# Router from unscaled rows, its broadcasts in two parts, and the first expert loaded in six pieces

## The reference

```
x = x + merged @ w_out
h = rmsnorm(x, g_ffn)                  # x * rsqrt(mean(x*x) + eps) * g
g_prob = softmax(h @ w_rg + b_rg)      # 4 groups; the best one
e_sel  = (h @ w_re + b_re)[group]      # 8 experts of that group
p_e, e_idx = top_k(softmax(e_sel), 2)  # two experts a row, shares scaled to sum 1
for e in range(32):
    hid = silu(h @ w_gate[e]) * (h @ w_up[e])          # 1024 -> 512
    y  += (hid * dense_w[:, e:e+1]) @ w_down[e]        # 512 -> 1024
x = x + y
```

## Time and profile before

| | before |
|---|---|
| median of 3 runs | 1783.94 us (1783.86 to 1784.62) |
| the profiled execution: its time | 1780.57 us |
| its span, first to last instruction | 1778.8 us |
| TensorE busy | 1538.4 us (86%) |
| VectorE busy | 945.3 us (53%) |
| ScalarE (ACT) busy | 633.7 us (36%) |
| bytes moved, mean rate | 407.85 MB, 229 GB/s |
| experts' gate/up loads: number, size, median from issue to landing | 32, 4096 KB, 37.9 us |
| mean granted TensorE clock | 0.937 |

### The profile page before, as it was taken

The page is one execution under the profiler, slowest core; times in us unless marked ns, Lnnn a source line. Parts: engine busy times, 40 slices in busy tenths (PEclk is TensorE's granted clock), DMA queues, the critical chain, the costliest instruction groups (busy, mean ns, idle before and its releaser), DMA issues.

```text
span 1778.8 us, 30446 instructions
## 1 busy us (share of the span) xinstructions
PE 1538.4 (86%) x12249; PEld 1257.9 (71%) x12250; DVE 945.3 (53%) x1717; ACT 633.7 (36%) x1026; POOL 58.5 (3%) x71
## 2 busy tenths in 40 slices
PE   7999997999999999997999997996859666666666
PEld 7999886799989999885899986885744333333233
DVE  5666686466566666775665667764643222222222
ACT  5444564444444444563544457434310000000000
POOL 1000020000000000010200000000000000000000
PEclk9999998999999999998999998998979988888888
DMA  9555362265565554550555543442099999999996
GB/s 310 188 188 186 127 223 83 72 213 172 188 200 159 193 184 165 169 184 26 184 189 183 189 165 101 134 151 77 15 418 393 430 430 431 431 430 432 434 428 297
DMA packets 147225, 407.85 MB, mean 229 GB/s; under 512 B 5216, under 2 KB 98768, under 8 KB 138976
## 3 DMA queue, kind: packets, MB, share of 16 engines
q1 hardware_dynamic: 145888, 404.31, 61.3%
q0 software_dynamic: 1280, 2.75, 0.7%
HBM read 406.00 MB, written 1.05 MB: 229 GB/s over the span
## 4 chain that ended last, share of the span: by engine, by line
PE 60%; DMA 19%; DVE 9%; issue 5%; ACT 5%; POOL 1%; SPq 0%; POOLq 0%; DVEq 0%; ACTq 0%
DMA expert_gu<-in_exp_gu 19%; PE bank L1869 17%; PE bank L1870 17%; PE bank L1871 17%; PE bank L2448 4%; DVE wlo L1128 2%; ACT whi L702 2%; POOL small L627 1%; ACT prob L811 1%; PE bank L2464 1%; PE bank L2203 1%; DVE x L1185 1%; PE bank L2411 1%; ACT xn L716 1%; ACT hhi L710 0%
## 5 line engine op out<-in xcount | busy, mean ns | idle before, releaser
L1128 DVE TENSOR_TENSOR wlo<-raw,whi 128x1024 fp32r<-128x1024 f32 (+1 forms) x396 | 449.5, 1183 | 150.6 <-ACT whi L702 149.8
L1869 PE MATMUL bank<-hhi,whi 128*128 128x256 f32 x1504 | 427.7, 284 | 8.7 <-DVE hlo L1166 4.3
L1870 PE MATMUL bank<-hlo,whi 128*128 128x256 f32 x1504 | 426.6, 284 | 0.0
L1871 PE MATMUL bank<-hhi,wlo 128*128 128x256 f32 x1504 | 426.6, 284 | 0.0
L702 ACT ACTIVATE whi<-raw 128x1024 fp32r<-128x1024 f32 (+1 forms) x396 | 382.3, 1019 | 92.6 <-PE bank L1871 92.5
L1869 PEld LDWEIGHTS bank<-hhi,whi 128*128 128x128 f32 x1504 | 289.4, 192 | 13.0 <-issue 5.2
L1870 PEld LDWEIGHTS bank<-hlo,whi 128*128 128x128 f32 x1504 | 289.6, 193 | 3.1
L1871 PEld LDWEIGHTS bank<-hhi,wlo 128*128 128x128 f32 x1504 | 289.5, 192 | 0.0
L2448 PE MATMUL bank<-expert_gu,h_e 128*32 128x256 f32 x2112 | 169.9, 492 | 130.6 <-DMA expert_gu<-in_exp_gu 126.4
L2448 PEld LDWEIGHTS bank<-expert_gu,h_e 128*32 128x32 f32 x2112 | 84.6, 140 | 215.8 <-issue 194.4
L1817 DVE SCALAR_TENSOR_TENSOR e_sg<-e_th,bank 128x128 f32<-128x128 f32 x33 | 9.5, 287 | 305.2 <-ACT e_th L1084 305.2
(11 more groups left out here) (358 smaller groups left out, 1652.2 us busy)
## 6 DMA issues: line engine op xcount, KB each, us to landing
expert_gu<-in_exp_gu SPq DMA_DIRECT2D x32, 4096.0 KB, 37.9
expert_dn<-in_exp_dn SPq DMA_DIRECT2D x32, 2048.0 KB, 38.7
raw<-in_ffn_w_gate SPq DMA_DIRECT2D x44, 1024.0 KB, 5.5
raw<-in_ffn_w_up SPq DMA_DIRECT2D x44, 1024.0 KB, 7.4
raw<-in_ffn_w_down SPq DMA_DIRECT2D x44, 1024.0 KB, 4.9
raw<-in_w_in SPq DMA_DIRECT2D x36, 1024.0 KB, 5.1
raw<-in_w_o SPq DMA_DIRECT2D x8, 1024.0 KB, 5.3
raw<-in_w_out SPq DMA_DIRECT2D x4, 1024.0 KB, 5.2
```

The costliest lines, as they stand in the source:

```text
L1128: nc.vector.tensor_tensor(slot_view(wlo, slot, src), src, slot_view(whi, slot, src).bitcast(F32), ALU.subtract).then_inc(lo_ready, inc)
L1869: nc.tensor.matmul(o, sh, mh, start=first, stop=False, skip_group_check=shared)
L1870: nc.tensor.matmul(o, sh, ml, start=False, stop=False, skip_group_check=shared)
L1871: return nc.tensor.matmul(o, sl, mh, start=False, stop=last, skip_group_check=shared)
```

## The change

- SP no longer waits for all six raw tiles to be free before it loads expert 0. It loads it in six pieces of 1 MB (four of gate/up, two of down), each as soon as the job that lay in that place has been split. Expert 2's down tile goes behind the first piece, its gate/up tile ahead of the last.
- The rows that TensorE turns for the router are those of x, neither scaled nor multiplied by the gain. The gain is multiplied into `w_router` instead, and the row's scale is applied to the logits. `hcol` is copied by ACT for t = 0 and by VectorE for t = 1. The squares go to a tile of their own (`sink`). `xn`, which the gather needs, is x times gain from VectorE and then scaled by ACT.
- The shares' four `diag` operations are on ACT, directly after the picks, and have a matmul of their own; the slots' four stay on VectorE, behind `take`, and their matmul stands behind the first gather. Both matmuls use one bank.
- `w_router`'s product with the gain and two memsets (`give`, `y_sb`) stand ahead of the last update of x.

The core of the diff:

```diff
@@ -592,15 +596,39 @@
-                if plan:
-                    for k in range(2):
-                        for w in last_use(last, batches(last) - 2 + k):
-                            sp.wait_ge(lo_ready, w)
-                expert(0, 0, None)
+                st, b, m = plan[last]
+                def piece(job):
+                    n = 3 * ((b + job // 3) % 2) + job % 3
+                    sp.wait_ge(lo_ready, mid_pos(last, job, 1) + 1)
+                    t, name, o, done = (expert_gu[0], "exp_gu", n, gu_landed[0]) if n < 4 else (expert_dn[0], "exp_dn", n - 4, down_landed[0])
+                    dst = t[:].rearrange("p k q n -> p (k q n)") if n < 4 else t[:].rearrange("p k n -> p (k n)")
+                    c = slice(o * 2 * HALF, (o + 1) * 2 * HALF)
+                    sp.dma_start(dst[:, c], a[name][0, :, c]).then_inc(done if o == 0 else consts_loaded, 16)
+                def down_part(e, j):
+                    src = a["exp_dn"][e:e + 1, :, :].rearrange("e p n -> p (e n)")
+                    sp.dma_start(expert_dn[j][:].rearrange("p k n -> p (k n)"), src).then_inc(down_landed[j], 16)
+                def gate_up_part(e, j):
+                    src = a["exp_gu"][e:e + 1, :, :].rearrange("e p n -> p (e n)")
+                    sp.dma_start(expert_gu[j][:].rearrange("p k q n -> p (k q n)"), src).then_inc(gu_landed[j], 16)
+                jobs = 3 * batches(last)
+                piece(jobs - 6)
+                sp.wait_ge(yt_ready, 4)
+                down_part(2, 2)
+                for job in range(jobs - 5, jobs - 1):
+                    piece(job)
...
-                expert(2, 2, None)
+                gate_up_part(2, 2)
+                piece(jobs - 1)
...
-                expert(1, 1, None)
+                gate_up_part(1, 1)
+                down_part(1, 1)
...
@@ -1064,18 +1092,31 @@
-                for g in range(4):
-                    t, h = g // 2, g % 2
-                    act.wait_ge(tr_ready, n + g + 1)
-                    nc.scalar.activation(hcol[:, 4 * h:4 * h + 4, t * P:(t + 1) * P],
-                                         TR[g][:].rearrange("p (k c) -> p k c", c=P), ACT.Copy).then_inc(hhi_ready, 1)
-                act.wait_ge(glogits_ready, 1)
-                nc.scalar.activation(g4[:, :, 1, :], g4[:, :, 0, :], ACT.Exp).then_inc(gexp_ready, 1)
-                act.wait_ge(elogits_ready, 1)
-                nc.scalar.activation(x8[:, :, 1, :], x8[:, :, 0, :], ACT.Exp).then_inc(eexp_ready, 1)
-                act.wait_ge(rows_done, 1)
-                for h in range(2):
-                    nc.scalar.activation(rows4[:, 2 * h:2 * h + 2, :].rearrange("p v c -> p (v c)"), bank[6 + h][:],
+                for t in range(T):
+                    act.wait_ge(x_ready, 4 * i + 2 * t - 2)
+                    if t:
+                        act.wait_ge(squares_ready, 2 * i + 1)
+                    nc.scalar.activation(sink[:], x[:, t, :], ACT.Square, accum_out=small[:, 0, t:t + 1]).then_inc(squares_ready, 1)
+                    for h in range(2 if t == 0 else 0):
+                        act.wait_ge(tr_ready, n + h + 1)
+                        nc.scalar.activation(hcol[:, 4 * h:4 * h + 4, 0:P], TR[h][:].rearrange("p (k c) -> p k c", c=P),
+                                             ACT.Copy).then_inc(hhi_ready, 1)
+                act.wait_ge(root_ready, roots_by(i) + 1)
+                act.wait_ge(xn_ready, T)
+                for t in range(T):
+                    nc.scalar.activation(xn[:, t, :], xn[:, t, :], ACT.Identity, scale=nr[:, 0, t:t + 1]).then_inc(xn_ready, 1)
+                act.wait_ge(expin_ready, 1)
+                nc.scalar.activation(g4[:, :, 1, :], g4[:, :, 0, :], ACT.Exp).then_inc(expout_ready, 1)
+                act.wait_ge(expin_ready, 2)
+                nc.scalar.activation(x8[:, :, 1, :], x8[:, :, 0, :], ACT.Exp).then_inc(expout_ready, 1)
+                act.wait_ge(picks_ready, 1)
+                for v_ in range(2):
+                    for t in range(T):
+                        ins = nc.scalar.activation(diag[:, 2 * (2 + v_) + t, :], ident[:], ACT.Identity, scale=one[:, t, 10 + v_:11 + v_])
+                ins.then_inc(expout_ready, 1)
+                for o in range(2):
+                    act.wait_ge(rows_done, o + 1)
+                    nc.scalar.activation(rows4[:, 2 - 2 * o:4 - 2 * o, :].rearrange("p v c -> p (v c)"), bank[7][:],
...
@@ -1688,16 +1731,19 @@
-                update_x(i, 0.5)
-            def norm_rows(i):
-                dve.wait_ge(squares_ready, 2 * i + 2)
-                r = small[:, 3, 0:T]
-                rsqrt([mean_eps(0, T, D)], T, r)
+                if not moe:
+                    update_x(i, 0.5)
+                    return
+                dve.wait_ge(route_loaded, 80)
+                nc.vector.tensor_tensor(w_router[:], w_router[:], gcols[:, i + 1, :].rearrange("p (k o) -> p k o", o=1).broadcast_to([P, KC, LOGITS]),
+                                        ALU.mult)
+                nc.vector.memset(give[:], 0.0).then_inc(give_ready, 1)
+                nc.vector.memset(y_sb[:], 0.0).then_inc(y_copied, 1)
...
-                    nc.vector.scalar_tensor_tensor(xn[:, t, :], x[:, t, :], r[:, t:t + 1], gain[:],
-                                                   ALU.mult, ALU.mult).then_inc(xn_ready, 1)
+                    update_row(i, 0.5, t)
+                    dve.wait_ge(x_ready, 4 * i + 2 * t + 2)
+                    nc.vector.tensor_tensor(xn[:, t, :], x[:, t, :], gain[:], ALU.mult).then_inc(xn_ready, 1)
...
@@ -1721,15 +1767,21 @@
-                dve.wait_ge(route_loaded, 80)
+                n = turned(i)
+                for h in range(2):
+                    dve.wait_ge(tr_ready, n + 2 + h + 1)
+                    V.tensor_copy(hcol[:, 4 * h:4 * h + 4, P:S], TR[2 + h][:].rearrange("p (k c) -> p k c", c=P)).then_inc(hlo_ready, 1)
+                dve.wait_ge(squares_ready, 2 * i + 2)
+                root([mean_eps(0, T, D)])
+                dve.wait_ge(root_ready, roots[0])
...
-                link(V.tensor_tensor(logits[:], bank[4][:, 0:T * LOGITS].rearrange("p (t n) -> p t n", t=T),
-                                     b_router[:].rearrange("p (o n) -> p o n", o=1).broadcast_to([P, T, LOGITS]), ALU.add))
+                link(*[V.scalar_tensor_tensor(logits[:, t, :], bank[6][:, t * LOGITS:(t + 1) * LOGITS], nr[:, 0, t:t + 1], b_router[:],
+                                              ALU.mult, ALU.add) for t in range(T)])
...
-                V.tensor_tensor(g4[:, :, 0, :], gl, value(0).broadcast_to([P, T, NG]), ALU.subtract).then_inc(glogits_ready, 1)
-                dve.wait_ge(gexp_ready, 1)
+                V.tensor_tensor(g4[:, :, 0, :], gl, value(0).broadcast_to([P, T, NG]), ALU.subtract).then_inc(expin_ready, 1)
+                dve.wait_ge(expout_ready, 1)
...
@@ -1786,10 +1838,6 @@
-                for v, col in enumerate((2, 3, 10, 11)):
-                    for t in range(T):
-                        ins = V.tensor_scalar(diag[:, 2 * v + t, :], ident[:], one[:, t, col:col + 1], None, ALU.mult)
-                ins.then_inc(diag_ready, 1)
...
@@ -1807,6 +1855,10 @@
+                for v, col in enumerate((2, 3)):
+                    for t in range(T):
+                        ins = V.tensor_scalar(diag[:, 2 * v + t, :], ident[:], one[:, t, col:col + 1], None, ALU.mult)
+                ins.then_inc(diag_ready, 1)
...
@@ -2384,18 +2432,20 @@
-                    pe.wait_ge(xn_ready, t + 1)
+                    pe.wait_ge(x_ready, 4 * (i - 1) + 2 * t + 2)
...
-                                                      xn[:, t, (4 * h + k) * P:(4 * h + k + 1) * P], ident[:])
+                                                      x[:, t, (4 * h + k) * P:(4 * h + k + 1) * P], ident[:])
...
-                pe.wait_ge(hhi_ready, turned(i) + 4)
-                pe.wait_ge(route_loaded, 80)
-                for t in range(T):
+                for t in range(T):
+                    if t == 0:
+                        pe.wait_ge(hhi_ready, turned(i) + 2)
+                    else:
+                        pe.wait_ge(hlo_ready, turned(i) + 2)
...
-                        ins = nc.tensor.matmul(bank[4][:, t * LOGITS:(t + 1) * LOGITS], hcol[:, k, t * P:(t + 1) * P],
+                        ins = nc.tensor.matmul(bank[6][:, t * LOGITS:(t + 1) * LOGITS], hcol[:, k, t * P:(t + 1) * P],
...
@@ -2420,11 +2470,14 @@
-                pe.wait_ge(diag_ready, 1)
-                for h in range(2):
-                    ins = nc.tensor.matmul(bank[6 + h][:], ones, diag[:, 4 * h:4 * h + 4, :].rearrange("p v c -> p (v c)"),
-                                           start=True, stop=True)
-                ins.then_inc(rows_done, 1)
+                def rows(o):
+                    nc.tensor.matmul(bank[7][:], ones, diag[:, 4 - 4 * o:8 - 4 * o, :].rearrange("p v c -> p (v c)"),
+                                     start=True, stop=True).then_inc(rows_done, 1)
```

(8 more changed lines are left out.)

36 lines of the change are left out of this document (18 added, 18 removed).

## The result

| | before | after |
|---|---|---|
| median, the runs made for the comparison | 1783.9 us (1780.96 to 1784.62, 4 runs) | 1770.76 us (1769.9 to 1771.65, 4 runs) |
| ratio to before, 95% interval | | 0.9929, 0.9912 to 0.9947 |
| the profiled execution | 1780.57 us | 1769.9 us |
| its span | 1778.8 us | 1768.1 us |

The kernel is faster by 0.7%.

The account below looks back on a forecast made before the run. Expert loads at full DMA rate bound the kernel, so its end follows the fourth expert's load. Gain to the gather 12.6 us, part given back, sum 10.0: median 1783.94 - 10.0 = 1773.9 us, range 1770.8 to 1777.2.

Parts of the forecast that it names:

- Sum: First expert's product done at 1327.0 instead of 1337.06 us, a total gain of 10.0 us.
- rival 1: Clock already high at the gather, so product done at 1324.5: gain 12.6 us, 1771.3 us; chance 0.2.
- The end moves one for one with the fourth load: The kernel's end shifts as much as the fourth expert's load start, while the load queue never runs dry.
- Second bound: First three experts' loads end at about 1334.5 us; a faster router alone would gain at most 3.6 us.
- Early load: Expert 0 loaded in pieces as splits finish; first three experts' loads land by 1315 us instead of 1334.5.
- Rival 3: An early piece waits in SP's order, old load bound stays: gain at most 3.6 us, 1780.3 us; chance 0.04.
- Rival 5: Slower: early transfers stretch the mixer through shared SBUF; a stretch of a third gives 1788 us; chance 0.03.
- Router: Router from unscaled rows: group exponential at 1305.1 us instead of 1312.13, gaining 7.0 us.
- Gather: With the broadcasts apart, gather at 1318.55 us instead of 1331.12: gain up to there 12.6 us.
- Given back: Slots' matmul between gather and first product, at low clock: product starts at 1322.6, takes 4.4 us, ends 1327.0.
- Rival 2: All slow, the first product too at 6.60 us: done at 1329.2, gain 7.8 us, 1776.1 us; chance 0.09.
- The clock: TensorE at low clock for gather (2.14 us) and slots' matmul (1.89), near high for the first product (4.4).

Follow-up runs that it names:

- e6: Changed kernel with eight linked copies added on VectorE ahead of `rel`, to make the router later by 2.5 us: 1775.41 us, ratio 0.9963.
- e5: Changed kernel with spare matmuls keeping TensorE busy, 14 ahead of the counts and 7 behind the shares' broadcast: 1769.25 us, ratio 0.9927.
- e1: Changed kernel with the old loads, so new router and broadcasts only: 1778.22 us, ratio 0.9969 to before.
- e10: Changed kernel with three spare matmuls behind the shares' broadcast only, none ahead of the counts: 1771.43 us, ratio 0.9932.
- e8: Repeat of e5, the changed kernel with both sets of spare matmuls: 1769.21 us, ratio 0.992.
- e3: Changed kernel with the broadcasts together again, all eight `diag` operations ahead of `rel`, gather behind both row copies: 1776.7 us, ratio 0.9963.
- e0: The kernel before, unchanged, run again beside itself: 1783.58 us, ratio 0.9998.
- e2: The kernel before with the early load alone, old router and broadcasts kept: 1784.31 us, ratio 1.0006.
- e4: Changed kernel with the router from scaled rows as before, early load and broadcasts apart kept: 1779.31 us, ratio 0.9977.
- e7: The changed kernel, unchanged, run again: 1771.85 us, ratio 0.9943 to before.
- e9: Changed kernel with the 14 spare matmuls ahead of the counts only: 1772.33 us, ratio 0.9935.
- e11: The kernel of e3 with spare matmuls, 14 ahead of the counts and 7 behind them: 1774.77 us, ratio 0.9953.

## Why the prediction was right, point by point

- **Sum.** 10.0 us predicted, 10.5 at the load and 10.6 at the store by distances, 10.7 between profiled executions. The forecast of 1773.9 us was 3.1 above the first measured median (1770.76) and 2.1 above the repeat (1771.85). The first median stands right at the fast end of the stated range (1770.8), 0.04 us beyond it, and nearer to rival 1's 1771.3 than to the forecast: by the time alone, rival 1 would look better. It is the rows that tell the two apart. The prediction added the 3.4 us by which the profiled execution was under the median, as if the kernel made them; scatter ahead of the router makes such an offset.
- **The end moves one for one with the fourth load.** Right: e6 and e5 from both sides, 3.0 to 3.15 and 2.5 to 2.5. The last expert's product adds up to 1.0 us of its own clock (5.35 to 6.34).
- **Second bound, 3.6 us.** Right, 4.1 in e1. What makes the 0.5 above it wasn't tested.
- **Early load.** Pieces from 1255.39 to 1289.29, expert 2's gate/up at 1285.21, the DMA engines empty from 1316; predicted 1289.3, 1285 and 1315. Rival 3 falls. Rival 5 falls with the mixer's 11.93 us for 57 matmuls at 342 GB/s, and with the 43.78 to 43.84 us from the splits of job 24 to the mixer's end in all fourteen profiles, with early pieces or without.
- **Router.** 7.0 predicted; the group exponential stands 6.94 us behind the mixer against 14.16, so 7.2. It starts right after ACT's second scaling (2.19 us for two, where 2.0 was taken), as predicted; but the scaling's end, 1304.83, is not shown to be the bound, since VectorE's `g` ends at 1304.85. The prediction had VectorE's step end 0.4 us ahead of the scaling (1304.7 and 1305.1). How the gain divides among the router's rearrangements wasn't tested.
- **Gather.** 12.6 predicted; 20.37 against 33.15 is 12.8.
- **Given back.** Gather to first product 3.87 us where 4.03 was taken, product 4.32 where 4.4 was. Each term here is right within 0.2; all errors point to the same side and make the 0.5 us of the sum. Rivals 1 and 2 needed 1.07 or 6.60 in these rows and fall. Rival 1's price was too high: it left the slots' matmul out between gather and product. e10, with the high clock from the gather on, has 3.09 us there and not 2.27, and its load is 12.0 us earlier than before, not 12.6.
- **The clock.** The prediction read it from rows as a price of broadcasts apart. e5, e8 and e10 confirm it. The Trainium skill's page "TensorE: Matmul & The Clock Gate", section "Part 1: The HAM clock gate", has the half rate as the default, which only sustained activity releases; the trace agrees in direction (0.50 in counts, gather and slots' matmul, 1.00 once these had run without a pause). Rival 2's use of it was too dark: the product ran most of its 4.32 us at 1.00.

**Where the clock changed.** What the prediction didn't see is how much of this is luck of place. Where a stretch of 1 us holds one change between 0.50 and 1.00, its mean tells when. Before, e3, and after:

```profile
1330.00:1331.00 1.00, 0.00 (x0) 0.00 (x0) 0.00 (x0) 0.98 (x2) 0.00 (x0) 0.78 0.96 410
```

```profile
1330.00:1331.00 1.00, 1.00 (x20) 0.55 (x16) 0.00 (x0) 0.00 (x0) 0.00 (x0) 0.71 0.00 0
```

```profile
1323.00:1324.00 1.00, 1.00 (x20) 0.54 (x16) 0.00 (x0) 0.00 (x0) 0.00 (x0) 0.71 0.00 0
```

By this estimate the clock rises at 1330.44 before, while TensorE stands idle between broadcasts and gather, and at 1330.58 in e3, 4.0 us into the product. Counted from the mixer's end these are 32.5 and 32.4 us, and e0, e2 and e4 rise at 32.5 too, although e3's work stands 7 us earlier than that of before. After, e1, e7 and e9 rise at 25.6 to 25.7, e6 at 29.1, e10 at 18.8. e9 falls at 18.8 and e11 at 25.6. In these profiles the clock changed at the same few distances from the mixer's end, and the work did not move them. The product's time follows from it:

| kernel | product starts, us from the mixer's end | clock rises | product, us |
|---|---|---|---|
| e4 | 31.42 | 32.5 | 4.16 |
| after | 24.24 | 25.6 | 4.32 |
| e6 | 26.72 | 29.1 | 4.81 |
| e9 | 23.21 | 25.7 | 4.84 |
| e3 | 28.44 | 32.4 | 5.59 |

Each is 3.66 us plus about half of the part ahead of the rise. So the 4.4 us that the prediction chose between 3.67 and 6.60 came out because the rise fell 1.4 us into the product, which no term of it works out. The broadcasts apart are worth 5.5 us at the load against e3, whose clock stays low (34.27 to 28.79), and 3.5 with the old router, where the joint broadcasts are followed by the high clock (e2 to e4, 39.29 to 35.81).

What stays open: why the clock rose behind the joint broadcasts in three profiles with the old router and not in e3, where the same work stands 7 us earlier to these moments. The idle stretch before the counts also differs, 6.81 us in e3 and 5.83 before. No run varied either alone.

## What to carry to other kernels

Where two bounds end within a few microseconds of each other, price each edit against both: here one part was worth 4.1 us alone, the other nothing, and both together 10.6. To judge a change of a few microseconds under a scatter of three, compare the distance between a row ahead of the change and the row that the end hangs on; it repeated within 0.11 us here. A short idle stretch of TensorE ahead of a critical product can cost more than itself: here 2.52 us of it left gather, slots' matmul and product slow. Work without an effect placed in it (2.03 us) brought the load forward by 1.45 us, but the end by 0.33 only; 14 and 7 spare matmuls brought both forward by 2.5. And an estimate of a product that starts at the low clock needs the place of the next rise, not only the length of the work ahead of it.

## What the hardware showed that was not expected

- The same TensorE work with the same gaps got different clocks in two kernels (the gather 1.07 us in three profiles with the old router and joint broadcasts, 1.93 in the one of e3); the changed kernel's repeat had the same clock as its first profile (1.94 and 1.93). The changes stood at the same distances from the mixer's end, though that end itself moved by 3.3 us between profiles.
- The clock also fell in the middle of work. Before, the router's matmuls run from 1306.99 to 1311.36 without a pause, at 1.00 until about 1309.96 and at 0.50 from there on; the same matmuls in the changed kernel kept 1.00 throughout (3.66 us against 4.37).
- A faster clock uncovered other time: 0.95 us of "issue" ahead of the product appeared as soon as the matmul ahead of it took 1.12 in place of 2.08 us.
- The last product of the program, always behind a wait of 3.9 to 6.8 us for its transfer, took from 5.14 to 6.34 us among these profiles, against 3.66 at the high clock.
